# Two chained transformer blocks in fp32: feature-major activations, staggered bias rows and key tiles of 96, 96, 80

## The reference

```python
def first_block(x, meta_tokens, ...):          # 272 rows: meta + x
    hn = rmsnorm(h, pre_norm_g[layer])
    qa, ka, va, ga, qb, kb, vb, gb = jnp.split(hn @ w_in, ...)
    ya = gqa_axial_mixer(qa, ka, va, ...) * silu(ga)   # 8 heads, 2 key heads, rope
    yb = diff_attn_mixer(qb, kb, vb, ...) * silu(gb)   # 8 heads, two softmaxes, alibi
    h = h + rmsnorm(concat(ya, yb) @ w_out, post_norm_g)
    return h[:, N_META:, :]

def second_block(x, ..., rel_bias, ...):
    z = rms_norm(x, norm_mix) @ w_in           # q, k, v, u, gate_a, gate_b
    y_a = chunked_rel_attention(q, k, v, rel_bias)     # 16 heads of 64
    y_b = multiscale_pool(u, pool_w, pool_scale)
    x = x + (gate_a * (y_a @ w_branch_a) + gate_b * (y_b @ w_branch_b)) @ w_out
    x = x + swiglu(rms_norm(x, norm_ffn), w_gate_up, w_down)
    return rms_norm(x, norm_final)
```

## Time and profile before

| | |
|---|---|
| time, median of 3 runs | 1838.07 us (1836.72 to 1841.25) |
| profiled execution | 1839.43 us |
| its span | 1837.2 us |
| TensorE busy | 1802.5 us, 98% |
| VectorE, ScalarE, GpSimd busy | 1105.6, 811.9, 158.5 us |
| DMA | 325.62 MB, mean 177 GB/s |

### The profile page before, as it was taken

The page is one execution under the profiler, slowest core; times in us unless marked ns, Lnnn a source line. Parts: engine busy times, 40 slices in busy tenths (PEclk is TensorE's granted clock), DMA queues, the critical chain, the costliest instruction groups (busy, mean ns, idle before and its releaser), DMA issues.

```text
span 1837.2 us, 24794 instructions
## 1 busy us (share of the span) xinstructions
PE 1802.5 (98%) x9992; PEld 1548.8 (84%) x9992; DVE 1105.6 (60%) x1315; ACT 811.9 (44%) x1134; POOL 158.5 (9%) x165
## 2 busy tenths in 40 slices
PE   8999999999898999999999999999999999999997
PEld 8998767888797788888888888888888888888886
DVE  5545755455564556567777556665665665666666
ACT  5334455544452444444444444444343444444343
POOL 1004455000000005000000000000000000000000
PEclk9999999999898999999999999999999999999999
DMA  8554333355479544555665555555555555555552
GB/s 296 172 171 137 128 116 137 115 183 188 156 176 284 167 138 135 163 177 183 186 195 192 184 183 206 192 193 187 183 185 190 194 184 183 188 197 186 183 184 91
DMA packets 255823, 325.62 MB, mean 177 GB/s; under 512 B 5857, under 2 KB 191729, under 8 KB 255473
## 3 DMA queue, kind: packets, MB, share of 16 engines
q1 hardware_dynamic: 251408, 318.08, 52.5%
q10 hardware_dynamic: 4336, 6.44, 2.0%
HBM read 319.25 MB, written 5.24 MB: 177 GB/s over the span
## 4 chain that ended last, share of the span: by engine, by line
issue 62%; PE 29%; POOL 4%; DMA 2%; ACT 1%; DVE 1%; POOLq 0%; SPq 0%; DVEq 0%
PE acc L483 4%; PE acc L485 4%; PE acc L484 4%; PE acc L521 3%; DMA raw<-w_in 2%; PE acc L509 2%; PE acc L510 2%; PE acc L508 2%; PE acc L522 2%; PE acc L495 1%; PE acc L496 1%; PE acc L497 1%; POOL ybuf L1959 1%; PE scores L599 1%; PE aux L633 1%
## 5 line engine op out<-in xcount | busy, mean ns | idle before, releaser
L1372 DVE TENSOR_TENSOR wlo<-raw,whi 128x1024 fp32r<-128x1024 f32 x592 | 736.5, 1245 | 589.4 <-ACT whi L1009 588.3
L1009 ACT ACTIVATE whi<-raw 128x1024 fp32r<-128x1024 f32 x592 | 625.9, 1059 | 762.6 <-PE acc L522 443.2
L521 PE MATMUL acc<-hboth,whi 128*128 128x512 f32 x2176 | 771.3, 399 | 7.9 <-DVE wlo L1372 7.9
L522 PE MATMUL acc<-hboth,wlo 128*128 128x256 f32 x2176 | 609.6, 280 | 0.0
L521 PEld LDWEIGHTS acc<-hboth,whi 128*128 128x128 f32 x2176 | 409.8, 188 | 109.9 <-DVE wlo L1372 8.3
L522 PEld LDWEIGHTS acc<-hboth,wlo 128*128 128x128 f32 x2176 | 411.5, 189 | 0.4
L483 PE MATMUL acc<-whi,fhi 128*128 128x512 f32 x352 | 137.2, 390 | 0.0
L485 PE MATMUL acc<-whi,flo 128*128 128x512 f32 x352 | 137.1, 389 | 0.0
L484 PE MATMUL acc<-wlo,fhi 128*128 128x512 f32 x352 | 137.0, 389 | 0.0
L509 PE MATMUL acc<-xboth,whi 128*128 128x272 f32 x320 | 92.5, 289 | 0.0
L508 PE MATMUL acc<-xboth,whi 128*128 128x272 f32 x320 | 92.3, 289 | 0.0
(11 more groups left out here) (266 smaller groups left out, 2380.9 us busy)
## 6 DMA issues: line engine op xcount, KB each, us to landing
raw<-w_in SPq DMA_DIRECT2D x116, 1024.0 KB, 5.5
raw<-w_gate_up SPq DMA_DIRECT2D x88, 1024.0 KB, 4.9
raw<-w_down SPq DMA_DIRECT2D x44, 1024.0 KB, 5.1
raw<-w_out SPq DMA_DIRECT2D x32, 1024.0 KB, 5.1
raw<-w_branch_a SPq DMA_DIRECT2D x8, 1024.0 KB, 5.7
raw<-w_branch_b SPq DMA_DIRECT2D x8, 1024.0 KB, 5.7
rel_scratch<-reltab ACTq DMA_DIRECT2D x1, 3072.0 KB, 33.4
xres<-x SPq DMA_DIRECT2D x4, 512.0 KB, 9.7
```

Of the source, the lines that this page charges most:

```text
L521: nc.tensor.matmul(o.rearrange("p (s t) -> p s t", t=TOK), hi, both[:, :, kt, 0:TOK], start=kt == 0, stop=False)
L522: done = nc.tensor.matmul(o[:, 0:TOK], lo, both[:, 0, kt, 0:TOK], start=False, stop=kt == tiles - 1)
L1009: nc.scalar.activation(whi[:, j % 4], raw[:, j // 2, 2 * (j % 2):2 * (j % 2) + 2, :], ACT.Copy).then_inc(hi_ready, 1)
L1372: nc.vector.tensor_tensor(wlo[:, j % 4], raw[:, j // 2, 2 * (j % 2):2 * (j % 2) + 2, :], whi[:, j % 4].bitcast(F32), ALU.subtract).then_in ...
```

## The change

Three parts.

1. The host lays out x and the meta rows feature-major (`x_t`, `meta_t`). Five loads bring x to `xt`, and ACT and DVE split it from there; TensorE's transposes of x and of the meta rows are gone. x is still needed in rows (`xres`), for the squares and the residual, and is loaded in one transfer behind the weights of quad 0. The squares of x move from pieces 5 and 6 of quad 0 to pieces 0 and 1 of quad 1, DVE's variance from piece 0 to piece 1. The first weight load is cut in two, and so is the first split; TensorE's warm-up has 15 matmuls in one row.
2. The host lays out the padded table 128 times (`rel_rows`, 3 MB). ACT's queue reads 8 heads at c = 1 and 8 at c = 2, with the same shortened pitch. `reltab`, POOL's copy and the scratch are gone.
3. The 272 keys stand as tiles of 96, 96 and 80. `vb` and `va` have three tiles; `vbm` and `vam` are gone.

```diff
+KEY_TILES = ((0, 96), (96, 96), (192, 80))
+XT_PARTS = ((0, 2), (2, 4), (4, 8), (8, 12), (12, 16))
...
-        vb = place("vb", [P, TT, 1024], at=o_1 + 16896)
-        vbm = place("vbm", [META, 1024], at=o_1 + 25088)
+        vb = place("vb", [P, 3, 1024], at=o_1 + 16896)
...
+                if (b, half) != (KVA, 0):
+                    for at, tiles in ((0, KEY_TILES[0:2]), (1, KEY_TILES[2:3])):
+                        if at:
+                            bank = aux_bank()
+                        for i, (k0, rows) in enumerate(tiles):
+                            for c in range(2):
+                                done = nc.tensor.transpose(bank[0:rows, i * 256 + c * P:i * 256 + (c + 1) * P], src[:, c, k0:k0 + rows], ident)
...
-                        for k in range(2):
-                            nc.tensor.transpose(bank[:, k * P:(k + 1) * P], p[:, k * P:(k + 1) * P], ident)
-                        nc.tensor.transpose(bank[0:META, TOK:TOK + P], p[:, TOK:KEYS], ident).then_inc(aux_ready, 1)
+                        for k, (k0, rows) in enumerate(KEY_TILES):
+                            done = nc.tensor.transpose(bank[0:rows, k * P:(k + 1) * P], p[:, k0:k0 + rows], ident)
...
-                        for k in range(2):
-                            nc.tensor.matmul(o, w[:, k * P:(k + 1) * P], v[:, k, c], start=k == 0, stop=False)
-                        done = nc.tensor.matmul(o, w[0:META, TOK:TOK + P], vm[0:META, c], start=False, stop=True)
+                        for k, (_, rows) in enumerate(KEY_TILES):
+                            done = nc.tensor.matmul(o, w[0:rows, k * P:(k + 1) * P], v[0:rows, k, c], start=k == 0, stop=k == 2)
...
-            for _ in range(8):
+            for _ in range(15):
                 nc.tensor.matmul(acc[1][0][:], zeros[:, 0:P], zeros[:], start=True, stop=True)
-            pe.wait_ge(start_in, 16)
-            for s in range(2):
-                pe.wait_ge(x_in[0], 16)
-                transpose_group(G_X + s, xres, 2 * s)
-
-            for _ in range(8):
-                nc.tensor.matmul(acc[1][0][:], zeros[:, 0:P], zeros[:], start=True, stop=True)
...
-                    if b == 0 and j in (1, 2, 4):
-                        pe.wait_ge(x_in[j // 2 + 1], 16)
-                        for s in (j // 2 * 2 + 2, j // 2 * 2 + 3):
-                            transpose_group(G_X + s, xres, 2 * s)
-                    if b == 0 and j == 6:
-                        meta_transposes()
...
+            x_part(0)
+            sp.dma_start(gcol, t["start_c"][:, P:P + 56]).then_inc(start_in, 16)
+            sp.dma_start(raw[:, 0, 0:2], first[0][:, 0:2]).then_inc(first_in, 16)
+            x_part(1)
+            sp.dma_start(raw[:, 0, 2:4], first[0][:, 2:4]).then_inc(raw_in[0], 16)
+            for u in range(1, 4):
+                x_part(u + 1)
+                sp.dma_start(raw[:, u], first[u]).then_inc(raw_in[u], 16)
+            sp.dma_start(metat[:], t["meta_t"]).then_inc(metat_in, 16)
+            sp.dma_start(ident, t["start_c"][:, 0:P]).then_inc(ident_in, 16)
+            sp.dma_start(xres[:], t["x"][0].rearrange("(i p) d -> p i d", p=P)).then_inc(xres_in, 16)
...
+                    act.wait_ge(first_in, 16)
+                    nc.scalar.activation(whi[:, 0, 0], raw[:, 0, 0], ACT.Copy).then_inc(first_hi, 1)
+                    nc.scalar.activation(whi[:, 0, 1], raw[:, 0, 1], ACT.Copy).then_inc(hi_ready, 1)
...
+                    act.wait_ge(x_in[XT_PART[s]], 16)
+                    for k in range(2):
+                        done = nc.scalar.activation(hi[:, k, :], xt[:, 2 * s + k, :], ACT.Copy, scale=gcol[:, g + k:g + k + 1])
...
-                            nc.scalar.activation(pt[:, i, 0:TOK], bank[:, 0:TOK], ACT.Copy)
-                            done = nc.scalar.activation(pt[0:META, i, TOK:TOK + P], bank[0:META, TOK:TOK + P], ACT.Copy)
+                            nc.scalar.activation(pt[0:96, i, 0:2 * P], bank[0:96, 0:2 * P], ACT.Copy)
+                            done = nc.scalar.activation(pt[0:80, i, 2 * P:3 * P], bank[0:80, 2 * P:3 * P], ACT.Copy)
...
-                    if b == 0 and j in (5, 6):
-
-                        i = j - 5
-                        nc.scalar.activation((qtb, qta)[i][:].rearrange("p a b -> p (a b)"), xres[:, i, :], ACT.Square,
-                                             accum_out=ss[:, i:i + 1]).then_inc(squares1, 1)
+                    if b == 1 and j < 2:
+                        act.wait_ge(xres_in, 16)
+                        nc.scalar.activation((vb, qta)[j][:].rearrange("p a b -> p (a b)")[:, 0:D], xres[:, j, :], ACT.Square,
+                                             accum_out=ss[:, j:j + 1]).then_inc(squares1, 1)
...
-                        act.dma_start(bass.AP(tensor=scratch, offset=0, ap=[[REL, HEADS2], [row, P], [1, REL]]),
-                                      dims(reltab[:], [0, P], [1, REL])).then_inc(rel_out, 16)
...
-                        act.dma_start(bias2[:], bass.AP(tensor=scratch, offset=127,
-                                                        ap=[[row - 1, P], [REL, HEADS2], [1, TOK]])).then_inc(bias2_in, 16)
+                        h = 8 * (c - 1)
+                        act.dma_start(bias2[:, h:h + 8, :], bass.AP(tensor=t["rel_rows"].tensor, offset=127 + h * REL,
+                                                                    ap=[[HEADS2 * REL - 1, P], [REL, 8], [1, TOK]])).then_inc(bias2_in, 16)
...
-                    if b == 1 and j == 0:
+                    if b == 1 and j == 1:
                         dve.wait_ge(squares1, 3)
```

More of the change, by code:

```diff
@@ L94 @@
 START1, START2 = 43, 8 * 21 + 6
+XT_PARTS = ((0, 2), (2, 4), (4, 8), (8, 12), (12, 16))
+XT_PART = {s: c for c, (lo, hi) in enumerate(XT_PARTS) for s in range(lo // 2, hi // 2)}
 def start_of(n):
@@ L218, in build @@
         ylo = place("ylo", [P, 8, TOK], F32R, at=o_1 + 8192)
-        metax = place("metax", [META, D], at=o_ybuf)
-        mtmp = place("mtmp", [P, KT, META], at=o_ybuf + 8704)
+        xt = place("xt", [P, KT, TOK], at=o_ybuf)
+        metax = place("metax", [META, D], at=o_1 + 8192)
+        metat = place("metat", [P, KT, META], at=o_1 + 37376)
+        mtmp = place("mtmp", [P, KT, META], at=o_1 + 38400)
         turn = [place("turn0", [P, 2, KEYS], at=o_ybuf), place("turn1", [P, 2, KEYS], at=o_s)]
@@ L486, in piece, with piece_turned @@
                 done.then_inc(piece_used, 1)
-            def piece_turned(j, banks, hi_of, lo_of):
+            def piece_turned(j, banks, hi_of, lo_of, first=None):
                 for k in range(2):
                     kt = 2 * j + k
+                    if first is not None:
+                        pe.wait_ge(*first[k])
                     for c in range(4):
@@ L627, in attend @@
                     h = n // 2 if is_b(n) else (n - 16) // 4
-                    v, vm = (vb, vbm) if is_b(n) else (va, vam)
+                    v = vb if is_b(n) else va
                     c = slice(h * HD, (h + 1) * HD)
@@ L938, in _, with x_part @@
             w1, w2, wgu, wdn = t["w_in"][0], t["w_in_2"][0], t["w_gate_up_2"][0], t["w_down_2"][0]
[L939 to L945, removed]
+            first = [w.rearrange("(k p) n -> p k n", p=P) for w in column_block(w1, W1[0][2] * CW)]
+            def x_part(c):
+                lo, hi = XT_PARTS[c]
+                sp.dma_start(xt[:, lo:hi, :], t["x_t"][:, lo:hi, :]).then_inc(x_in[c], 16)
+            x_part(0)
[9 more added lines that the diff above has]
+            sp.dma_start(xres[:], t["x"][0].rearrange("(i p) d -> p i d", p=P)).then_inc(xres_in, 16)
             for name, dst in (("rope_t", rope[:]), ("dist_t", dist[:])):
@@ L1099, in take_rows @@
                     at = part * CW + half * 256
[L1100 removed]
+                    dst = vb[:, :, at:at + 256]
                 elif half == 0:
@@ L1103, in take_rows @@
                 else:
-                    dst, dst_meta = va[:], vam[:]
+                    dst = va[:]
+                if (b, half) != (KVA, 0):
+                    act.wait_ge(aux_ready, use["rows", n])
+                    nc.scalar.activation(dst[0:96, 0:2, :], aux[(use["rows", n] - 1) % 2][0:96, :].rearrange("p (i c) -> p i c", c=256), ACT.Copy)
+                    act.wait_ge(aux_ready, use["last rows", n])
+                    nc.scalar.activation(dst[0:80, 2, :], aux[(use["last rows", n] - 1) % 2][0:80, 0:256], ACT.Copy).then_inc(rows_taken, 1)
+                    return
                 act.wait_ge(aux_ready, use["rows", n])
@@ L1370, in split @@
                 g = 8 * q + j
+                if isinstance(g, int) and g == 0:
+                    for k, (half_hi, half_lo) in enumerate(((first_hi, first_lo), (hi_ready, lo_ready))):
+                        dve.wait_ge(half_hi, 1)
+                        nc.vector.tensor_tensor(wlo[:, 0, k], raw[:, 0, k], whi[:, 0, k].bitcast(F32), ALU.subtract).then_inc(half_lo, 1)
+                    return
                 dve.wait_ge(hi_ready, g + 1)
@@ L1380, in stat_group @@
```

(10 more changed lines are left out.)

78 lines of the change are left out of this document (38 added, 40 removed).

## The result

The changed kernel takes 1820.3 us (median of four runs, 1818.93 to 1823.38), the kernel before, with a fourth run beside it, 1839.05 us: a ratio of 0.9905, 95% interval 0.9893 to 0.9916. The forecast was 1822 us in a range of 1811 to 1833.

The account below looks back on a forecast made before the run. TensorE, busy in 98% of the span, was taken as the bound; -10.7 (bias) - 12.2 (key tiles) + 6.7 (start) = -16.2, so 1838.1 became 1822 us, range 1811 to 1833 (its own 1817 to 1827).

Parts of the forecast that it names:

- Part 1: Second block's bias: the 7.9 us wait for split weights and 2.8 us of slow matmuls behind it go, -10.7 us.
- Rival C: Second block's stop stays because staggered reads hold up weights as the write did; 1833 us, chance 0.08.
- Part 2: Attention key tiles: 32 16-row matmuls each save 0.42 us, less 1.2 in the rope-chain wait, -12.2 us.
- Rival B: Attention: TensorE pays for every change of row count, +6.7 us instead of a gain; 1841 us, chance 0.06.
- Part 3: Start: the early first matmul is lost to waits behind x's second copy in SP's queue, +6.7 us.
- L: Start: landing of block 1's first weights, forecast at 38.1 us, bounds 35.5 to 40.
- from squares to broadcast: Start: ACT's splits and squares, variance, POOL's powers and broadcast put piece 9 at L + 11.1 = 49.2 us.
- +5.1 + 1.6: Start: piece 9 begins 5.1 us later than before, plus 1.6 us for slow matmuls after TensorE's idle time.
- A: Start doesn't lose: x's second copy finds idle share, L is 34 or less; 1815 or 1807 us, chance 0.14.
- D: Start: x's second copy is carried by few of the 16 engines, taking 41 us; 1858 us, chance 0.05.

Follow-up runs that it names:

- part 1 alone: Kernel before with only the bias change: rows read from the host's layout in two 1 MB loads, no scratch write; 1827.16 us, ratio 0.9935.
- the run with 64 rows: Changed kernel with key tiles of 104, 104 and 64 instead of 96, 96 and 80; 1830.59 us, ratio 0.9955 to the kernel before.
- the tiles alone: Kernel before with only the keys cut into tiles of 96, 96 and 80; 1827.76 us, ratio 0.9937.
- kernel with nine loads moved: Changed kernel with rope, dist and seven small loads moved behind quad 1's third weight load; 1815.71 us, ratio 0.9876 to the kernel before.
- squares ahead: Kernel with nine loads moved, plus squares of x's first half ahead of ACT's first quad 1 split, variance back at piece 0; 1814.25 us, ratio 0.9863.
- seven loads moved: Changed kernel with only the seven small broadcast loads moved behind quad 1's third weight load; 1818.70 us, ratio 0.9894 to the kernel before.

## Why the prediction was right, point by point

**Part 1** stood at -10.7. Alone it brings 10.6 in its stretch of the trace. The write is the cause, as forecast, and its price comes back whole when it is put back (11.1 in the trace); that its 16 partitions make it slow, as the prediction's wording has it, is not shown. The reads beside the weights cost nothing: 9.6 and 7.0 us to landing in the changed kernel, 10.6 and 5.5 with part 1 alone, and no wait in either. Rival C is out.

**Part 2** stood at -12.2, as 32 x 0.42 less 1.2. Alone it measured -11.6, in the trace 10.9. The mechanism held, and the run with 64 rows shows it. Two sizes were off and cancelled. The price of a matmul is 0.39: the prediction took the first L483 behind an item at 0.23 us from the clean case, but behind a full-form group too it takes 0.31 (307.76 to 308.07), so that 0.08 an item had nothing to do with the form. And the wait for the rope chain ate 0.5 instead of 1.2. Sum 32 x 0.39 - 0.5 = 12.0. The trace's 10.9 is 1.1 less. That difference was not found, but it is no larger than what two traces with the same tiles differ by in this stretch (240.6 us in the changed kernel, 239.4 with the tiles alone). Rival B is out.

**Part 3** stood at +6.7 and is the term that was mis-sized: +3.5 alone. L was forecast at 38.1 and was 37.1; the first matmul 8.1 and 7.6; the wait ahead of piece 8 about 8 and 6.3 us. The term "from squares to broadcast", L + 11.1, was 9.5. Of the missing 1.6 us, 1.75 are POOL's two powers, 2.09 us where rows 10 show 3.84. For this reason, and because piece 8 took 5.2 us at its low clock where the prediction had about 4.4, TensorE idled 0.9 us instead of 3 ahead of the broadcast. The slow matmuls came ahead of it, behind the wait for weights, where they cost nothing (40 to 44 us at 0.50), and the 1.6 us of them that the sum had behind it did not come (44 to 47 at 1.00). So +5.1 + 1.6 became +2.5 in the trace of before as it stood. But the step also trusted one profile of a start that varies: two others of the same start begin piece 9 at 41.7 and 41.9, against which the changed kernel's 46.61 is 4.8 to 5.0 later. Rivals A and D are out: the second copy did not find room, nor did it run on few engines (16.4 us for 2 MB).

**The sum** of the three parts measured alone is -12.0 - 11.6 + 3.5 = -20.1; together 18.75 by the medians, 15.4 to 19.7 by the interval. The 18.75 are on the scale of medians and the parts on that of ratios, where the whole is 17.5; so the parts add up to 2.6 us more than the whole, which their intervals allow. The forecast of -16.2 erred on the start by 3.2 and on the bias and tiles by less than the measurement tells.

The prediction worked in the profiled execution, and there its -16.2 met 15.9 (1837.2 to 1821.3 us). That close a hit is partly luck. Cut at the same events, the two traces differ by +2.5 at the start, -9.7 in the attention of block one, -1.1 between that and the second block's first 512-column matmuls, -10.6 at the bias, and +3.0 behind the second block's first scores. The last is none of the three parts (the last section has it); without it the traces would be 18.9 us apart, 2.7 more than forecast.

## What to carry to other kernels

A matmul of few rows between full ones is dear by where it stands, not by its work: here 0.39 us each with 16 rows or 64, gone by cutting 272 keys into 96, 96, 80. Activations that arrive ready-made start TensorE earlier, but the gain is only as long as the queue behind: put ahead of the next weights nothing that is needed later, and count small loads beside their bytes (here about 0.36 us each). DMA engines can be fully busy and move less than half of what they can (148 to 184 GB/s against 361 here); look at GB/s beside the share.

## What the runs showed that was not expected

TensorE has two paces at granted clock 1.00. In the stretch of 144 us with `aboth` the same 256-column and 512-column matmuls run at one of two speeds. By line, in 830 to 960 us (the view names the group by `hboth`, which alternates with `aboth` and `bboth`), first the kernel with nine loads moved, then the one with the squares ahead:

```profile
L528 PE MATMUL acc<-hboth,whi 128*128 128x512 f32 x192 | 66.7, 394 | 0.0
L529 PE MATMUL acc<-hboth,wlo 128*128 128x256 f32 x192 | 53.2, 277 | 0.0
```

```profile
L528 PE MATMUL acc<-hboth,whi 128*128 128x512 f32 x192 | 68.0, 399 | 0.0
L529 PE MATMUL acc<-hboth,wlo 128*128 128x256 f32 x192 | 53.9, 281 | 0.0
```

From the first to the last `aboth` matmul are 143.8 us in the one and 146.7 in the other, with no wait in either. Of the eleven profiles six have 143.8 to 143.9 and five 146.6 to 146.7, whatever the edit. Nothing else differs behind the second block's first scores: from there to the end are 1220.4 or 1220.5 us in the same six and 1223.4 or 1223.5 in the same five. The profile of before has the fast pace, that of the changed kernel the slow one, which hides 3.0 us of its gain and fits its being the slowest of its four runs. VectorE's splits take 1222 and 1221 ns and ACT's 1061 in both, so those two are not slower. The cause was not found. Differences of 3 us between two profiles of this kernel are not evidence.

POOL's two powers took 3.84 us or 2.08. In the old start (before, the bias rows alone, and the tiles alone) they take 3.84 to 3.85, and three splits of VectorE, without a gap, begin 0.2 us ahead of them. In the new start they take 2.08 or 2.09, and the splits begin 0.45 us behind them (changed kernel: POOL at 43.45, VectorE at 43.90; squares ahead: 34.65 and 35.10). Splits run beside POOL in both. That it depends on which of the two begins first fits all of these; it was not tried.

The length of an idle time of TensorE did not decide alone whether the clock fell: with seven loads moved, 2.82 us ahead of piece 8 were followed by a granted clock of 0.64 in 36 to 39 us, and 1.32 us ahead of the broadcast by 0.50 in 45 to 47; with nine moved, 2.85 us ahead of the broadcast were followed by 1.00 in 41 to 44.
